# A four-stage decoder trunk: channel sums of the norms by a ones matmul per token half, and one norm begun under the last value product

## The reference

```python
def rms_norm(x, g):
    return x * lax.rsqrt(jnp.mean(x * x, axis=-1, keepdims=True) + RMS_EPS) * g
def modulate(h, shift, scale):
    return h * (1 + scale) + shift
def swiglu(h, w_gate, w_up, w_down):
    return (silu(h @ w_gate) * (h @ w_up)) @ w_down

# layer 0
x = x + 0.5 * gate * swiglu(modulate(rms_norm(x)), ...)      # ffn0
x = x + gate * moba_mixer(modulate(rms_norm(x)), ...)        # mixA, woA
x = x + 0.5 * gate * swiglu(modulate(rms_norm(x)), ...)      # ffn1
# shared keys and values of three dilated branches
kv_bands = shared_kv_bands(modulate(rms_norm(x)), kv_w)      # kv
# layer 1: ffn2, mixB and woB (dilated_mixer), ffn3
return rms_norm(x, final_g)
```

## Time and profile before

| | us |
|---|---|
| median of 3 runs | 2713.72 |
| lowest and highest | 2708.33 to 2715.49 |
| profiled execution | 2703.8 |
| its span in the profile | 2702.1 |
| PE busy | 2485.3 (92%) |
| DVE busy | 1376.9 (51%) |
| ACT busy | 902.8 (33%) |
| POOL busy | 649.1 (24%) |

### The profile page before, as it was taken

One profiled execution on the slowest core, in us unless ns is written; L12 is line 12 of the kernel. 1 busy time (PEld: TensorE's weight loads), 2 busy tenths in 40 slices (PEclk: granted clock), 3 DMA queues, 4 the chain that ended last, 5 costly groups with the idle time before them and its releaser, 6 DMA issues. The chain is left out here.

```text
span 2702.1 us, 34855 instructions
## 1 busy us (share of the span) xinstructions
PE 2485.3 (92%) x12230; PEld 2078.6 (77%) x12230; DVE 1376.9 (51%) x1843; ACT 902.8 (33%) x1244; POOL 649.1 (24%) x356
## 2 busy tenths in 40 slices
PE   2999998888789999999999999997888989899998
PEld 2888877777678888779997888875777877788886
DVE  6666434566656664244335666325766655533322
ACT  2333223444533332221113333222544554333321
POOL 2222121433102221211111222112544540122221
PEclk9999998999689999989999999998999979899999
DMA  6555432433135554334444555434645441222232
GB/s 220 185 189 181 135 116 94 135 109 109 51 110 187 185 187 137 108 100 141 142 141 167 191 180 177 133 100 130 152 120 133 126 123 40 74 97 93 93 94 86
DMA packets 117535, 356.09 MB, mean 132 GB/s; under 512 B 14672, under 2 KB 23248, under 8 KB 117328
## 3 DMA queue, kind: packets, MB, share of 16 engines
q1 hardware_dynamic: 110544, 329.88, 39.5%
q0 software_dynamic: 6912, 25.17, 2.6%
HBM read 327.73 MB, written 27.26 MB: 131 GB/s over the span
## 5 line engine op out<-in xcount | busy, mean ns | idle before, releaser
L256 PE MATMUL ps<-h_hi,w_hi 128*128 128x512 f32 x2048 | 824.9, 403 | 38.1 <-DVE h_lo L585 25.2
L257 PE MATMUL ps<-h_lo,w_hi 128*128 128x512 f32 x2048 | 809.3, 395 | 0.0
L258 PE MATMUL ps<-h_hi,w_lo 128*128 128x512 f32 x2048 | 809.0, 395 | 0.0
L247 ACT CAST w_hi<-w_raw 128x1024 fp32r<-128x1024 f32 (+1 forms) x384 | 394.9, 1028 | 871.0 <-PE ps L258 868.2
L251 DVE TENSOR_TENSOR w_lo<-w_raw,w_hi 128x1024 fp32r<-128x1024 f32 x249 | 330.5, 1327 | 670.2 <-ACT w_hi L247 670.1
L251 POOL TENSOR_TENSOR w_lo<-w_raw,w_hi 128x1024 fp32r<-128x1024 f32 (+1 forms) x135 | 305.1, 2260 | 1378.1 <-ACT w_hi L247 1378.1
L256 PEld LDWEIGHTS ps<-h_hi,w_hi 128*128 128x128 f32 x2048 | 392.5, 192 | 145.4 <-issue 41.6
L258 PEld LDWEIGHTS ps<-h_hi,w_lo 128*128 128x128 f32 x2048 | 391.5, 191 | 84.8
L257 PEld LDWEIGHTS ps<-h_lo,w_hi 128*128 128x128 f32 x2048 | 393.0, 192 | 76.5
L256 PE MATMUL ps<-act_hi,w_hi 128*128 128x512 f32 x704 | 276.6, 393 | 6.4 <-POOL w_lo L251 6.3
L258 PE MATMUL ps<-act_hi,w_lo 128*128 128x512 f32 x704 | 274.2, 389 | 0.0
(11 more groups left out here) (84 smaller groups left out, 2776.2 us busy)
## 6 DMA issues: line engine op xcount, KB each, us to landing
w_raw<-gate_up SPq DMA_DIRECT2D x176, 512.0 KB, 3.7
ada_raw<-ada SPq DMA_DIRECT2D x160, 512.0 KB, 4.6
w_raw<-down SPq DMA_DIRECT2D x80, 512.0 KB, 3.6
w_raw<-kv_w SPq DMA_DIRECT2D x48, 512.0 KB, 3.5
w_raw<-mixa_w SPq DMA_DIRECT2D x32, 512.0 KB, 3.7
w_raw<-mixb_w SPq DMA_DIRECT2D x32, 512.0 KB, 3.8
k_raw<-kb SPq DMA_DIRECT2D x64, 192.0 KB, 5.0
q_raw<-qb SPq DMA_DIRECT2D x64, 192.0 KB, 4.0
```

What stands on the lines that cost most here:

```text
L247: nc.scalar.copy(w_hi[:, slot, 0:n], w_raw[:, slot, 0:n]).then_inc(w_hi_done, 1)
L256: nc.tensor.matmul(out_ap, l_hi, r_hi, start=start, stop=False, skip_group_check=skip)
L257: nc.tensor.matmul(out_ap, l_hi, r_lo, start=False, stop=False, skip_group_check=skip)
L258: return nc.tensor.matmul(out_ap, l_lo, r_hi, start=False, stop=stop, skip_group_check=skip)
```

## The change

- **Sums and reciprocals.** The squares' sum is multiplied by a full matrix of ones, one matmul per half of the tokens (256). The result already lies along the tokens on all partitions. ScalarE takes the root of each half from PSUM into a new SBUF tile `rinv` (128x512), VectorE the reciprocal of each half in place. `diag`, `rb` and the 128x4 tiles go. The multiply of k = 0 is made in two halves, one after each reciprocal, its `h_hi` and `h_lo` too.
- **The last pair of a residual phase.** Its two tiles are finished one after the other in the last unit, so that the first is updated, squared and added while the second is still multiplied; the second tile is updated, squared and added in halves of the tokens. In the down products the last pair takes its units in another order, TAIL_KS: the short one first.
- **Queues.** ScalarE's `w_hi` of the next phase's second unit moves from before the root to after `h_hi` of k = 0; its `w_lo` stays with GpSimd in mixA, kv and mixB and goes to VectorE, after `h_lo` of k = 1, in ffn1 and ffn3. VectorE's `w_lo` of the next phase's first unit moves behind the sums.
- **ffn2's norm** moves into the last turn of the kv phase: k = 0 to 3 once the first value unit has been used, k = 4 to 7 after the second. The last `v_copy` comes after all of it.
- The loops over pairs in the residual phases are unrolled. At the start of the program nothing stands between the two condition blocks any more.

The core of the diff (semaphore counts and renamings left out):

```diff
+TAIL_KS = (2, 4, 4, 4, 4, 4)
+HALF_T = S // 2
-        rb = ps[:, 4, :]
-        stat = ps[:, 5, 0:TT]
+        stat = [ps[:, 4, 0:HALF_T], ps[:, 5, 0:HALF_T]]
         def pe_stats(pe, r):
-            pe.wait_ge(sum_done, 9 * (r + 1))
-            for t in range(TT):
-                mm = nc.tensor.matmul(stat[:, t:t + 1], tmp[:, 2, t * P:(t + 1) * P], ones[:, 0:1],
-                                      start=True, stop=True)
-            mm.then_inc(stat_done, 1)
-            pe.wait_ge(diag_done, r + 1)
-            nc.tensor.matmul(rb, ones[:], diag[:].rearrange("p t n -> p (t n)"),
-                             start=True, stop=True).then_inc(rb_done, 1)
+            for half in range(2):
+                pe.wait_ge(sum_done, sums_before(r) + (9 + half if r else 9))
+                nc.tensor.matmul(stat[half], ones[:], tmp[:, 2, tokens(half)],
+                                 start=True, stop=True).then_inc(stat_done, 1)
...
+                if tail and j == len(ks) - 1:
+                    for n in range(2):
+                        for k4 in range(kn):
+                            mm = pe_k_half(bank, j % 2, k4, n, in_hi, in_lo, k + k4, last_k)
+                        if n == 0:
+                            mm.then_inc(half_done, 1)
+                    mm.then_inc(unit_used, 1)
+                    return
...
+        def pair_ks(ks, pair):
+            return TAIL_KS if pair == 3 and ks == DOWN_KS else ks
...
+        def act_rms(act, r):
+            for half in range(2):
+                act.wait_ge(stat_done, 2 * r + half + 1)
+                nc.scalar.activation(rinv[:, tokens(half)], stat[half], ACT.Sqrt, bias=eps[:, 0:1],
+                                     scale=1.0 / D).then_inc(rms_done, 1)
+        def dve_rinv(dve, r, half):
+            dve.wait_ge(rms_done, 2 * r + half + 1)
+            nc.vector.reciprocal(rinv[:, tokens(half)], rinv[:, tokens(half)]).then_inc(rinv_done, 1)
+        def dve_norm(dve, name, r, block, then={}):
+            h0 = h_count(name)
+            for half in range(2):
+                dve_rinv(dve, r, half)
+                dve.wait_ge(rinv_done, 2 * r + half + 1)
+                dve_scaled(dve, 0, tokens(half), 1)
+            dve_low(dve, name, block, 0, slice(0, 2), 1, 1)
+            dve_scaled(dve, 1, slice(0, S), 2)
+            dve_low(dve, name, block, 0, slice(2, 4), 2, 1)
+            dve_norm_rest(dve, name, block, range(2, KT), then)
...
         def act_residual(act, name, u0, p0, ks, r, res):
+            for pair in range(4):
+                u, p = u0 + n_u * pair, p0 + pair
+                stop = pair == 3 and name == "ffn3"
+                for j in range(n_u - 2 if stop else n_u - 1):
+                    w_split_hi(act, u + j + 2, j % 2, split_size(ks, pair, j + 2))
+                for j in range(2):
...
+                        nc.scalar.activation(tmp[:, j, at], x[:, n, at], ACT.Square).then_inc(sq_done, 1)
+                if pair < 3:
+                    w_split_hi(act, u + n_u + 1, (n_u - 1) % 2, split_size(ks, pair, n_u + 1))
...
         def dve_residual(...):
...
+                else:
+                    dve.wait_ge(half_done, res + 1)
+                    update(n, whole, x_first)
+                    add_square(n, whole, 7, 7)
+                    dve.wait_ge(unit_used, u + n_u)
+                    update(n + 1, tokens(0), x_first)
+                    update(n + 1, tokens(1), pair_free)
+                    add_square(n + 1, tokens(0), 8, 8)
+                    add_square(n + 1, tokens(1), 9, 9)
+                    if name != "ffn3":
+                        w_split_lo(dve, u + n_u, 0)
...
         def act_kv(act):
-            with act.Fori(0, G * NB) as i:
+            with act.Fori(0, G * NB - 1) as i:
                 for j in range(4):
                     w_split_hi(act, i * 4 + u0 + 2 + j, j % 2)
+            last = UNIT0["ffn2"] - 4
+            for j in range(3):
+                w_split_hi(act, last + 2 + j, j % 2)
+            act.wait_ge(unit_used, UNIT0["ffn2"] - 1)
+            act_norm(act, "ffn2", SUB_BLOCK[3], range(4))
+            w_split_hi(act, last + 5, 1)
+            act.wait_ge(unit_used, UNIT0["ffn2"])
+            act_norm(act, "ffn2", SUB_BLOCK[3], range(4, KT))
...
         def dve_kv(dve, col_n):
...
+            i = G * NB - 1
+            keys(i)
+            dve_gain(dve, SUB_BLOCK[3], 3, col_n)
+            dve.wait_ge(rope_done, rope_before("mixB"))
+            dve_scaled(dve, 0, slice(0, S), 2)
+            dve_scaled(dve, 1, slice(0, S), 2)
+            w_split_lo(dve, i * 4 + u0 + 4, 0)
+            dve_low(dve, "ffn2", SUB_BLOCK[3], 0, slice(0, 4), 2, 2)
+            dve_norm_rest(dve, "ffn2", SUB_BLOCK[3], range(2, 4))
+            dve.wait_ge(h_lo_done, h_count("ffn2") + 6)
+            dve_scaled(dve, 4, slice(0, S), 2)
+            w_split_lo(dve, i * 4 + u0 + 5, 1)
+            dve.wait_ge(unit_used, i * 4 + u0 + 4)
+            dve_norm_rest(dve, "ffn2", SUB_BLOCK[3], range(5, KT))
+            v_copy(dve, 2, i + 4)
...
-            act_norm(act, "mixA", SUB_BLOCK[1])
+            act_norm(act, "mixA", SUB_BLOCK[1], range(KT), {0: lambda: w_split_hi(act, UNIT0["mixA"] + 1, 1)})
...
-                if b == 0:
-                    dve_diag(dve, 0)
                 mod_store(dve, b)
...
-            dve_norm(dve, "ffn1", 2, SUB_BLOCK[2], 2, col + 4)
+            dve_norm(dve, "ffn1", 2, SUB_BLOCK[2], {2: lambda: w_split_lo(dve, UNIT0["ffn1"] + 1, 1)})
```

## The result

| | us |
|---|---|
| before, beside it | 2711.02 median (2707.55 to 2715.49) |
| after | 2743.57 median (2739.44 to 2747.63) |
| ratio | 1.0119, 95% interval 1.01 to 1.0137 |
| profiled execution, its span | 2741.07, 2739.3 |

What follows compares the result with a forecast made beforehand. TensorE was taken as the bound almost everywhere, so edits count only through its gaps or clock. The terms summed to +20.2 us on the 2713.7 us median, forecasting 2734 us, own range 2724 to 2743, wider range 2715 to 2746.

Steps and rivals of the forecast that it cites:

- Term 1: Norm chains: shorter by 0.8 us at kv with reciprocals of 2.3 us; five norms -4.6 us, final norm -0.4.
- Rival A: Wide reciprocal is cheap, 0.42 us instead of 2.3, so 14 give 26 us back: 2708 us; chance 0.13.
- Term 2: Norms of mixA, kv, mixB: GpSimd's later `w_lo` holds VectorE's multiplies through shared SBUF access; +5.8 us.
- Term 3: Last down pair of four FFNs: short unit first leaves TensorE waiting 2.9 us for GpSimd's `w_lo`; +11.0 us.
- Term 4: Half clock behind the four new down-pair gaps, 1.6 us each; +6.5 us.
- Term 5: ffn2's norm under the last value product: no gap before ffn2, but a wait after its first pair; +2.1 us.
- Term 6: First norm +0.8 us, its first matmul at 57.7; unrolled residual loops save 1 us; together -0.2 us.

Runs made afterwards that it cites:

- b_unroll: Kernel before with only TensorE's residual loop over down and output products written out: 2709.36 us, ratio 0.9998.
- p_tail: a_pad with the last down pair in the old order of units, the short one last: 2714.46 us, ratio 1.0014.
- a_pad: Changed kernel plus an unused 64-byte tile that puts act_hi, act_lo and the mixer tiles back at their old addresses: 2727.46 us, ratio 1.006.
- b_nop: Kernel before with 113 semaphore increments, which nothing waits for, ahead of VectorE's first weight split: 2716.76 us, ratio 1.0025.
- best_nop: a_pad with old down-pair order, `v_copy` earlier, `w_hi` before the root, and 8 idle VectorE increments ahead of the second mixer: 2700.04 us, ratio 0.9957.
- a_again: The changed kernel run once more, unaltered, for a second trace: 2735.78 us, ratio 1.0102.
- p_whi: a_pad with the second unit's `w_hi` split before the root again in mixA, kv and mixB: 2721.39 us, ratio 1.0049.
- p_vcopy: a_pad with the last `v_copy` moved ahead of the last three tiles of ffn2's norm: 2718.35 us, ratio 1.0037.
- b_shift: Kernel before plus an unused 64-byte tile ahead of the feed-forward and mixer tiles: 2714.91 us, ratio 1.0014.
- b_shift128: Kernel before plus an unused 128-byte tile ahead of the feed-forward and mixer tiles: 2721.82 us, ratio 1.0031.

## Why the prediction was right, and where it wasn't

The time came out 32.6 us above the kernel before, where 20.2 were forecast. The sign and most of the places are right, but that the time fell into the range is luck: the forecast's own terms came out at +7.6 together, and what brought the time up to the range was in none of them. Step by step, in microseconds:

| | forecast | shown | from |
|---|---|---|---|
| norm chains, five | -4.6 | -9.6 | traces |
| final norm | -0.4 | -1.5 | traces |
| first norm, unrolled loops | -0.2 | -1.1 | trace, b_unroll |
| GpSimd in the norms | +5.8 | +3.5 | trace |
| short unit first, four times | +11.0 | +10.4 | traces, p_tail |
| the clock behind it | +6.5 | +3.4 | trace |
| ffn2's norm | +2.1 | +2.5 | traces |
| address of `act_hi`, `act_lo` | none | +13.9 | traces (a_pad's ratio: 11.4) |
| place of VectorE's code, mixB | none | +6.5 | b_nop, best_nop |

The sum of the second column is +28.0, beside medians of +32.6 and +25.0 in the two comparisons of the same kernel. The traced executions are 37.3 us apart; the 4 us of the first group that I did not take apart and the 7.1 us of the last, which a_again has not, cover that difference with 2 us too many.

**Term 1, right in sign, too small.** The chains are shorter by 2.3 us at mixA, where I had 1.4, and by 1.7 to 1.9 at the other four, where I had 0.8. The mis-sized term is the reciprocal, all 14 of them:

```profile
L586 DVE RECIPROCAL rinv<-rinv 128x256 f32<-128x256 f32 x14 | 24.4, 1745 | 1.7 <-ACT rinv L581 1.2
```

1.745 us, not 2.3 (my slope itself gives 2.37), and two of them stand in each chain, so 1.1 us, all that is missing at kv. The two small rows from which I took the slope, 1 and 4 elements wide, gave 8.7 ns for each further element; over the whole width it is (1745 - 152) / 255 = 6.2. The Trainium skill, "VectorE: DVE Perf Modes", section "First, the fixed hardware budget", would have been nearer with its repeat count of 8: the estimate from it was 2.13 us, still 0.4 above the row. Rival A decided at 1.4 us and is out, but it was nearer than I said.

**Term 2, right, 2.3 us too high.** The mechanism is in kv's timeline above: `h_lo` takes 2.86 us beside GpSimd's 2.92, and ends 0.55 us after it, as `act_lo` does in the earlier trace rows. TensorE paid 0.93, 0.64 and 1.90 us of waits in mixA, kv and mixB. The Trainium skill, "GPSIMD Engine Reference", section "8. Key points", says that GpSimd contends with VectorE instructions of two SBUF inputs; the trace agrees, here (2.86 us) and in the split of the mixer's third head (2.72 us instead of 1.22). What I had not reckoned with: in the rows of that head the one that starts first is served first, so 0.2 us decides who pays. p_whi showed that the remedy that I had in mind for this term isn't one.

**Term 3, right.** Four waits of 2.79 to 2.80 us where 2.9 were forecast and 0.2 stood.

**Term 4, half.** The stretches behind two of the four waits in the kernel after (the clock is the third number from the end); the one from 1140.80 has 1.00 as well, the one from 2695.00 has 0.58:

```profile
406.20:409.60 3.40, 3.40 (x15) 2.77 (x16) 0.94 (x1) 0.00 (x0) 0.00 (x0) 1.00 0.72 219
...
1811.00:1814.40 3.40, 3.40 (x10) 2.64 (x11) 0.87 (x1) 0.00 (x0) 0.00 (x0) 0.57 0.74 231
```

Two of four fell to half clock. The gaps are alike to 0.01 us, so their length alone doesn't decide it. In a_again, with gaps of the same 2.79 and 2.80 us, it is the same two, the third and the fourth (0.58 and 0.70 in the 3.4 us behind the gap); in a_pad, with four of 2.87 us, it is the first, second and fourth (0.71, 0.55 and 0.57) and not the third. What decides is open; my 1.6 us for every gap was right for a gap that is hit (1.7) and wrong in taking all four.

**Term 5, right in all its steps:** no gap before ffn2, but one of 6.55 us after its first pair, on a `w_lo` of VectorE, which waited for the store of `v_copy` and then ran beside GpSimd's. TensorE resumed 0.2 us later than in the kernel before, where I had it 0.5 earlier, and the half clock behind it cost 2.4 us where I had 2.6. What the queue position cost is seen in p_vcopy: 7.1 us in the traces.

**Term 6** had the first norm 1.9 us too late (55.77 us instead of 57.7): 1.1 of it are the two reciprocals, and the first of them starts at 49.71, where I had let the chain begin at 50.4. The unrolled loops gave nothing that can be measured on TensorE, where I had put part of a microsecond's gain.

**The step that failed** is one that isn't written down: that what the diff doesn't touch keeps its time. Some 20 us of the loss came from code that the change leaves alone. It moved data by 64 bytes and an instruction stream by 113 instructions. The range held because the written terms cost 12.6 us less than forecast, 7 of these in the norms, which hid more than half of it.

## What to carry to other kernels

When tiles are removed, look at the addresses of what lies behind them. Compare the spacing of the same matmuls before and after, at full clock and without gaps, and if it has changed, put the old address back with padding before judging the change. Where two engines want SBUF within 0.2 us of each other, look at what either order costs; a few instructions that do nothing can settle which one it is. And order within a queue is where this change lost what its norms had won: with the units in the old order, the copy ahead of the norm, the padding and the eight increments it is 0.4% faster than the kernel before, not 1.2% slower; without the increments it was level with it. And a sum that comes out inside its range is no proof of its terms: check each against its own rows.

## What was unexpected of the hardware

- The spacing of 128x512 matmuls, three passes of fp32r, depends on where the moving tile lies in SBUF: 0.2267 us with `act_hi` at byte 105344 of the partition, 0.2290 at 105408 (b_shift), 0.2333 at 105280 (the change), and 0.229 and 0.238 in turn, 0.2333 on average, at 105472 (b_shift128). Which rule it follows is open, and whether only the matmuls' own reads are the cause wasn't tried.
- VectorE stood still for 0.35 to 0.37 us ahead of one instruction in the first pass of a program loop of 180 instructions, at a place that moved when 8 or 113 instructions were put ahead of it. What the engine did in that time isn't shown.
- A `TENSOR_SCALAR` of 128x64, one tensor input, took 3.31 us beside a GpSimd `TENSOR_TENSOR` of 3.41 that had begun 0.16 us earlier, against 0.25 us in the kernel before: an operation with a single tensor input is held too.
- A reciprocal costs 6.2 ns for each further element of a partition (1745 ns for 256, 152 for one), where an ordinary operation took 1.06.
